# Start addresses of activation tiles, small tiles, and the weight ring in a two-block transformer layer

## What is computed

```
block 1: z = rmsnorm(x) @ w_in                      # "in": 36 tiles of 128 columns
         conv branch (31 taps), short conv branch   # -> a, s
         x += (g_a * (a @ w_a_out) + g_b * (s @ w_b_out)) @ w_o        # "a_out", "b_out", "o"
         u = rmsnorm(x) @ w_up; x += (gelu(conv(u1)) * u2) @ w_down    # "up", "down", hidden f
         x += sigmoid(rmsnorm(x) @ w_ple_gate) * (p @ w_ple)           # "gate", "ple"
block 2: qkv = rmsnorm(x) @ w_in_2                  # "in2", then attention -> y
         x += rmsnorm(y @ w_out_2)                                     # "out2"
         u = rmsnorm(x) @ w_up_2; f = gelu(conv(u1)) * conv(u2)        # "up2"
         x += rmsnorm(f @ w_down_2)                                    # "down2"
```

## Time and profile before

| | us |
|---|---|
| timed runs: median (lowest to highest) of 3 | 823.68 (821.07 to 823.71) |
| the profiled execution | 822.88 |
| its span, first to last instruction | 821.1 |
| TensorE busy | 779.7 (95%) |
| VectorE, ScalarE, GpSimd busy | 600.5, 449.6, 264.9 |
| DMA | 135.44 MB, mean 165 GB/s |

### The profile page before, as it was taken

The page is one execution under the profiler, slowest core; times in us unless marked ns, Lnnn a source line. Parts: engine busy times, 40 slices in busy tenths (PEclk is TensorE's granted clock), DMA queues, the critical chain, the costliest instruction groups (busy, mean ns, idle before and its releaser), DMA issues.

```text
span 821.1 us, 16957 instructions
## 1 busy us (share of the span) xinstructions
PE 779.7 (95%) x5954; PEld 748.8 (91%) x5954; DVE 600.5 (73%) x1058; ACT 449.6 (55%) x756; POOL 264.9 (32%) x160
## 2 busy tenths in 40 slices
PE   5989899899999999999899999699999999999996
PEld 5889899899999999999899998699999999988885
DVE  5899976767888888434957686479999999973333
ACT  7444354556565655444655564586666666653431
POOL 0366644464122212345563011642112221222220
PEclk9999999899999999999989999989999999999999
DMA  8445454455555557545433332525555555565551
GB/s 281 141 155 179 161 192 130 133 181 181 191 180 190 180 198 247 178 148 167 135 122 111 104 103 79 179 84 175 181 182 184 188 181 179 204 203 187 181 173 51
DMA packets 37771, 135.44 MB, mean 165 GB/s; under 512 B 4448, under 2 KB 4704, under 8 KB 37728
## 3 DMA queue, kind: packets, MB, share of 16 engines
q1 hardware_dynamic: 37728, 134.86, 49.7%
HBM read 133.80 MB, written 1.05 MB: 164 GB/s over the span
## 4 chain that ended last, share of the span: by engine, by line
PE 52%; DVE 3%; POOL 2%; issue 1%; ACT 1%; DVEq 0%; ACTq 0%; POOLq 0%
PE bank L1618 13%; PE bank L1619 12%; PE bank L1620 12%; PE bank L1948 4%; PE bank L1950 4%; PE bank L1949 4%; POOL sumsq L540 1%; PE bank L1823 1%; PE bank L1822 1%; DVE tmp L1382 1%; POOL X L658 1%; PE bank L1832 1%; DVE w_lo L1024 1%; PE bank L1640 0%; PE bank L1848 0%
## 5 line engine op out<-in xcount | busy, mean ns | idle before, releaser
L1618 PE MATMUL bank<-h_hi,w_hi 128*128 128x256 f32 x1424 | 410.7, 288 | 22.1 <-DVE h_lo L1036 13.4
L1619 PE MATMUL bank<-h_lo,w_hi 128*128 128x256 f32 x1424 | 406.4, 285 | 0.0
L1620 PE MATMUL bank<-h_hi,w_lo 128*128 128x256 f32 x1424 | 406.2, 285 | 0.0
L527 POOL TENSOR_TENSOR w_lo<-raw,w_hi 128x1024 fp32r<-128x1024 f32 (+2 forms) x78 | 192.9, 2477 | 407.4 <-ACT w_hi L684 407.4
L684 ACT ACTIVATE w_hi<-raw 128x1024 fp32r<-128x1024 f32 (+2 forms) x246 | 261.9, 1067 | 87.5 <-PE bank L1950 43.2
L1618 PEld LDWEIGHTS bank<-h_hi,w_hi 128*128 128x128 f32 x1424 | 276.7, 194 | 29.2 <-issue 21.3
L1024 DVE TENSOR_TENSOR w_lo<-raw,w_hi 128x1024 fp32r<-128x1024 f32 (+1 forms) x168 | 218.6, 1302 | 109.8 <-ACT w_hi L684 109.7
L1619 PEld LDWEIGHTS bank<-h_lo,w_hi 128*128 128x128 f32 x1424 | 277.1, 195 | 0.0
L1620 PEld LDWEIGHTS bank<-h_hi,w_lo 128*128 128x128 f32 x1424 | 276.8, 194 | 0.0
L1064 DVE TENSOR_TENSOR bank<-bank,scales 128x256 f32<-128x256 f32 x124 | 53.1, 431 | 37.3 <-PE bank L1620 29.5
L1291 DVE TENSOR_TENSOR f_lo<-src,f_hi 128x256 f32 (+1 forms) x54 | 58.7, 1086 | 0.5 <-ACT f_hi L831 0.5
(11 more groups left out here) (198 smaller groups left out, 924.3 us busy)
## 6 DMA issues: line engine op xcount, KB each, us to landing
raw<-in_w_up SPq DMA_DIRECT2D x108, 512.0 KB, 3.3
raw<-in_w_in SPq DMA_DIRECT2D x54, 512.0 KB, 3.4
...
```

The costliest lines, as they stand in the source:

```text
L527: nc.gpsimd.tensor_tensor(w_lo[s][:, 0:n], raw[s][:, 0:n], w_hi[s][:, 0:n].bitcast(f32), ALU.subtract).then_inc(lo_ready[s], 1)
L1618: nc.tensor.matmul(ps, wh, hi[:, k, :], start=start and n == 0, stop=False)
L1619: nc.tensor.matmul(ps, wh, lo[:, k, :], start=False, stop=False)
L1620: last = nc.tensor.matmul(ps, wl, hi[:, k, :], start=False, stop=stop and n == len(ks) - 1)
```

## The change

`at` now starts at (16481 + 31) // 32 * 32 = 16512, a multiple of 128. Tiles of 1024 bytes or more start at multiples of 64, smaller ones at multiples of 32. The small tiles come first, zeros and unused become two more columns of ones_over. Behind them the rings start 32 bytes past a multiple of 64 (past=RING_PAST), and everything behind the rings at multiples of 64. In down2, from its fourth unit on (first_col), a unit is loaded, rounded, subtracted and read from column 8 of the ring, 32 bytes further; the first three units, whose rounding the loop of up2 does, stay at column 0. For that SP loads the first four units of down2 ahead of the loop and the other 28 in seven passes of it instead of eight. Worked out with the sizes above, the tiles start at:

| start modulo 128 | before | after |
|---|---|---|
| raw, w_hi, w_lo | 32 | 96 |
| the same in down2, from its fourth unit | 32 | 96 + 32 = 0 |
| X, branch, h, h2, src, tmp, sq, sumsq, last_sq, scales | 32 | 0 |
| ev, cg, cv, f, gate, conv, q, k, v, score | 64 | 0 |
| s, a, mix, p | 96 | 64 |
| y_a, y_b, y | 0 | 64 |
| ident | 0 | 0 |

```diff
@@ -52,6 +52,13 @@
 RING = 4
 SQ_RING = 6
 LEAD = 3
+
+RING_PAST = 32
+
+
+def first_col(u):
+
+    return RING_PAST // 4 if u >= UNIT0["down2"] + LEAD else 0
 
 
 def unit_blocks(u):
@@ -253,43 +260,27 @@
 
     with ExitStack() as ctx:
         sem = lambda name: ctx.enter_context(nc.semaphore(name))
-        at = [(nc.sbuf_base + 63) // 32 * 32]
-
-        def sb(name, shape, dt=f32, offset=None):
+        at = [(nc.sbuf_base + 31) // 32 * 32]
+
+        def aligned(offset, size):
+            step = 64 if size >= 1024 else 32
+            return (offset + step - 1) // step * step
+
+        def sb(name, shape, dt=f32, offset=None, past=0):
 
             size = 4 * math.prod(shape[1:])
-            size = (size + 31) // 32 * 32
             if offset is not None:
                 return nc.alloc_sbuf_tensor_at(name, shape, dt, offset=offset)
+            at[0] = aligned(at[0] - past, size) + past
             t = nc.alloc_sbuf_tensor_at(name, shape, dt, offset=at[0])
             at[0] += size
             return t
 
-        UNIT_MAX = max(b for _, _, b in PHASES) * P
-        raw = [sb(f"raw{i}", [P, UNIT_MAX]) for i in range(RING)]
-        w_hi = [sb(f"w_hi{i}", [P, UNIT_MAX], f32r) for i in range(RING)]
-        w_lo = [sb(f"w_lo{i}", [P, UNIT_MAX], f32r) for i in range(RING)]
-        X = sb("X", [P, DC, TOK])
-        branch = sb("branch", [P, DC, TOK])
-        h_hi = sb("h_hi", [P, DC, TOK], f32r)
-        h_lo = sb("h_lo", [P, DC, TOK], f32r)
-        h2_at = at[0]
-        h2_hi, h2_lo = sb("h2_hi", [P, DC, TOK], f32r), sb("h2_lo", [P, DC, TOK], f32r)
-
-        o_gain = sb("o_gain", [P, 2, D], offset=h2_at)
-        post_gain = sb("post_gain", [P, D], offset=h2_at + 8 * D)
-        o_sq = sb("o_sq", [P, HALF], offset=h2_at + 12 * D)
-        src = [sb(f"src{i}", [P, TOK]) for i in range(2)]
-        tmp = [sb(f"tmp{i}", [P, TOK]) for i in range(4)]
-        sq = [sb(f"sq{i}", [P, TOK]) for i in range(SQ_RING)]
-        sumsq = sb("sumsq", [P, 2, TOK])
-        last_sq = sb("last_sq", [P, 2, TOK])
-        scales = sb("scales", [P, 2, TOK])
-        gg = sb("gg", [P, DC])
         vec = sb("vec", [P, N_VEC])
         ident = sb("ident", [P, P])
+        gg = sb("gg", [P, DC])
         g_first = sb("g_first", [P, DC])
-        ones_over = sb("ones_over", [P, P + 1])
+        ones_over = sb("ones_over", [P, P + 3])
         lsum = sb("lsum", [P, 2])
         lexp = sb("lexp", [P, 2])
         neg_lam = sb("neg_lam", [P, 1])
@@ -301,7 +292,28 @@
         minus_half = sb("minus_half", [P, 8])
         o_ss = sb("o_ss", [P, 2, 2])
         o_ms, o_rstd = sb("o_ms", [P, 2]), sb("o_rstd", [P, 2])
-        zeros, unused = sb("zeros", [P, 1]), sb("unused", [P, 1])
+        zeros, unused = ones_over[:, P + 1:P + 2], ones_over[:, P + 2:P + 3]
+
+        UNIT_MAX = max(b for _, _, b in PHASES) * P
+        raw = [sb(f"raw{i}", [P, UNIT_MAX], past=RING_PAST) for i in range(RING)]
+        w_hi = [sb(f"w_hi{i}", [P, UNIT_MAX], f32r, past=RING_PAST) for i in range(RING)]
+        w_lo = [sb(f"w_lo{i}", [P, UNIT_MAX], f32r, past=RING_PAST) for i in range(RING)]
+        X = sb("X", [P, DC, TOK])
+        branch = sb("branch", [P, DC, TOK])
+        h_hi = sb("h_hi", [P, DC, TOK], f32r)
+        h_lo = sb("h_lo", [P, DC, TOK], f32r)
+        h2_at = at[0]
+        h2_hi, h2_lo = sb("h2_hi", [P, DC, TOK], f32r), sb("h2_lo", [P, DC, TOK], f32r)
+
+        o_gain = sb("o_gain", [P, 2, D], offset=h2_at)
+        post_gain = sb("post_gain", [P, D], offset=h2_at + 8 * D)
+        o_sq = sb("o_sq", [P, HALF], offset=h2_at + 12 * D)
+        src = [sb(f"src{i}", [P, TOK]) for i in range(2)]
+        tmp = [sb(f"tmp{i}", [P, TOK]) for i in range(4)]
+        sq = [sb(f"sq{i}", [P, TOK]) for i in range(SQ_RING)]
+        sumsq = sb("sumsq", [P, 2, TOK])
+        last_sq = sb("last_sq", [P, 2, TOK])
+        scales = sb("scales", [P, 2, TOK])
         ev = [sb(f"ev{i}", [P, TOK]) for i in range(4)]
         cg_pair = sb("cg", [P, 2 * TOK])
         cg, y_sq = [cg_pair[:, i * TOK:(i + 1) * TOK] for i in range(2)], cg_pair
@@ -312,8 +324,10 @@
             at_ = [start]
 
             def place(name, shape, dt=f32):
+                size = 4 * math.prod(shape[1:])
+                at_[0] = aligned(at_[0], size)
                 t = sb(name, shape, dt, offset=at_[0])
-                at_[0] += (4 * math.prod(shape[1:]) + 31) // 32 * 32
+                at_[0] += size
                 assert at_[0] <= nc.sbuf_usable_end, (name, at_[0])
                 return t
             return place
@@ -460,12 +474,12 @@
 
         @block.sync
         def _(sp):
-            def load(name, i, wait):
+            def load(name, i, wait, col=0):
 
                 s, n = wait
                 if n is not None:
                     sp.wait_ge(lo_ready[s], n)
-                sp.dma_start(raw[s][:, 0:BLOCKS[name] * P],
+                sp.dma_start(raw[s][:, col:col + BLOCKS[name] * P],
                              d["w_" + name][ds(i, 1)].rearrange("a p n -> (a p) n")
                              ).then_inc(raw_in[s], 16)
 
@@ -490,12 +504,15 @@
             sp.dma_start(sinks[:], d["sinks"].partition_broadcast(P)).then_inc(const_in, 16)
             for name, units, _ in PHASES:
                 base = UNIT0[name]
-                first = RING if name == "in" else 0
+                first = RING if name in ("in", "down2") else 0
+                for i in range(first if name == "down2" else 0):
+                    load(name, i, (slot(base + i), (base + i) // RING), first_col(base + i))
                 full = (units - first) // RING
                 with sp.Fori(0, full, 1) as it:
                     for j in range(RING):
                         i = first + RING * it + j
-                        load(name, i, (slot(base + first + j), it + (base + first + j) // RING))
+                        load(name, i, (slot(base + first + j), it + (base + first + j) // RING),
+                             first_col(base + first + j))
                 for i in range(first + RING * full, units):
                     load(name, i, (slot(base + i), (base + i) // RING))
                 if name == "gate":
@@ -523,9 +540,10 @@
 
                 if u < N_UNITS and on_pool(u):
                     s, n = slot(u), (blocks or unit_blocks(u)) * P
+                    cols = slice(first_col(u), first_col(u) + n)
                     pool.wait_ge(hi_ready, RING * it + (u + 1))
-                    nc.gpsimd.tensor_tensor(w_lo[s][:, 0:n], raw[s][:, 0:n],
-                                            w_hi[s][:, 0:n].bitcast(f32), ALU.subtract
+                    nc.gpsimd.tensor_tensor(w_lo[s][:, cols], raw[s][:, cols],
+                                            w_hi[s][:, cols].bitcast(f32), ALU.subtract
                                             ).then_inc(lo_ready[s], 1)
 
             def add_square(name, c):
@@ -678,10 +696,11 @@
             def round_unit(u, it=0, blocks=None):
 
                 s, n = slot(u), (blocks or unit_blocks(u)) * P
+                cols = slice(first_col(u), first_col(u) + n)
                 act.wait_ge(raw_in[s], 16 * it + 16 * (u // RING + 1))
                 if u >= RING:
                     act.wait_ge(unit_done, RING * it + (u - RING + 1))
-                nc.scalar.activation(w_hi[s][:, 0:n], raw[s][:, 0:n], ACT.Copy).then_inc(hi_ready, 1)
+                nc.scalar.activation(w_hi[s][:, cols], raw[s][:, cols], ACT.Copy).then_inc(hi_ready, 1)
 
             def ahead(u):
                 if u + LEAD < N_UNITS:
@@ -722,7 +741,7 @@
 
             def load_table(function):
 
-                nc.scalar.activation(unused[:], zeros[:], function)
+                nc.scalar.activation(unused, zeros, function)
 
 
             act.wait_ge(memset_done, 1)
@@ -1020,9 +1039,10 @@
                 if on_pool(u):
                     return
                 s, n = slot(u), (blocks or unit_blocks(u)) * P
+                cols = slice(first_col(u), first_col(u) + n)
                 dve.wait_ge(hi_ready, RING * it + (u + 1))
-                nc.vector.tensor_tensor(w_lo[s][:, 0:n], raw[s][:, 0:n],
-                                        w_hi[s][:, 0:n].bitcast(f32), ALU.subtract
+                nc.vector.tensor_tensor(w_lo[s][:, cols], raw[s][:, cols],
+                                        w_hi[s][:, cols].bitcast(f32), ALU.subtract
                                         ).then_inc(lo_ready[s], 1)
 
             def ahead(u):
@@ -1073,7 +1093,7 @@
                                         ).then_inc(op_lo, 1)
 
 
-            nc.vector.memset(zeros[:], 0.0).then_inc(memset_done, 1)
+            nc.vector.memset(zeros, 0.0).then_inc(memset_done, 1)
             nc.vector.memset(ones_over[:, 0:P], 1.0 / D_CONF).then_inc(memset_done, 1)
             nc.vector.memset(ones_over[:, P:P + 1], 1.0 / D).then_inc(memset_done, 1)
             for i in (0, 1):
@@ -1941,10 +1961,11 @@
             with pe.Fori(1, FC2 // 2, 1) as it:
```

(7 more changed lines are left out.)

28 lines of the change are left out of this document (14 added, 14 removed).

## The result

The changed kernel takes 808.9 us at the median of four runs (808.8 to 809.7), the kernel before 822.8 (821.1 to 823.7) beside it on the same chip. The ratio is 0.984, its 95% interval 0.9825 to 0.9855: faster by 13.9 us. The prediction was 815.3, its range 811.8 to 819.7. The profiled execution took 809.7 us, its span 807.8; the span of before was 821.1, so 13.3 us are to be found.

The account below looks back on a forecast made before the run. The prediction took TensorE, through the distance between matmul starts, to bound the kernel. 3456 h matmuls at 2.2 ns less gave 7.6 us, all else 0: 822.9 - 7.6 = 815.3 us, range 811.8 to 819.7.

Parts of the forecast that it names:

- What bounds the kernel: TensorE, busy 95% of the span; a stage lasts its matmul count times the distance between starts, which the addresses set.
- Nothing moves: Rival: the h stages' 2.2 ns come from something else and the addresses only coincide; 822.9 us, chance 0.12.
- equal remainders modulo 128: Matmuls whose moving tile and weights start alike modulo 128 are slow, 120.0 ns; unequal pairs are fast, 117.8 to 118.3.
- The price of h: Products moving h or h2 fall from 120.0 to 117.8 ns: 2.2 ns on 3456 matmuls, 7.6 us gained.
- down2, put at 0 with bounds of -4.4 and +6.6 ns: Second down projection, 512 moving columns: no net change taken, -1.7 to +2.5 us possible on 384 matmuls.
- the prediction's own sign of being wrong: A distance in down2 moved from 233.4 by more than 2 ns, listed among what would show the prediction wrong.
- The equal-pair reading: In down2 the new pair (0, 0) has equal starts, so it would cost 0.8 us (384 x 2.2 ns).
- "s", "a", "p" at the fast distance already: The stages moving s, a and p already run at the fast distance, so they gain 0.
- "down" at 0: The first down projection, moving f, already runs at the fast distance of 117.8 ns and gains 0.
- Other engines: VectorE, ScalarE and GpSimd durations stay, cost 0; in "up2" VectorE's 10.1 free us cover the 3.4 us gain.
- a worse pair: Rival: in all h stages the new pair takes 122.2 ns, 7.6 us more, 830.5 us; chance 0.04.
- The range: 811.8 to 819.7 us: below, down2's gain, shorter waits and spread; above, VectorE leading "up2", with 1 us of spread.

Follow-up runs that it names:

- e3: The kernel before with only the weight rings moved 32 bytes down: 811.5 us, ratio 0.990 to before.
- e4: The kernel before with all activation tiles (X and all behind it) moved 32 bytes up, rings unmoved: 810.9 us, ratio 0.987 to before.
- e5: Network left out, only products in groups of 24 at all pairs of start addresses modulo 256 in 32-byte steps: 113.3 to 120.0 ns for 256 columns.
- e9: Network left out, 48 products at six address pairs behind 12 at each of eight distances, or pauses: distance 192 took 113.3 or 117.8 ns.
- e1: The changed kernel without the column shift, down2's units all stored from column 0: 811.3 us, ratio 0.988 to before.
- e2: The changed kernel with RING_PAST = 0, the rings at a multiple of 64: 819.6 us, ratio 0.998 to before.

## Why the prediction was wrong in size and right in direction

- **What bounds the kernel**: right. PE is still busy for all of "up" and "up2", a stage is its count times the distance of starts, and the start addresses set it. "Nothing moves" is refuted by e3 and e4, which move one group of tiles by 32 bytes and win 10 us. The Trainium skill (SBUF — State Buffer, "Who interferes with whom") calls PE's read ports for the moving operand and for LDWEIGHTS independent and says that PE never waits on anyone; that gives no cost to the addresses, and these runs disagree: 113.3 to 120.0 ns in e5 with nothing exchanged but the two operands' starts. Where in the machine the time goes no run shows.
- **The class "equal remainders modulo 128"**: the step that failed. Four values, 120.0, 117.8, 117.9 and 118.3, were sorted into one slow and one fast class. They were four points of a table by the distance modulo 256, in which distance 96, unequal modulo 128, is as slow as 0 (e5, e9). Of what the class put at zero, "down2", "down" and "s" to "a_out" changed. That the direction came out right owes something to luck: by the class any unequal pair would have been fast, and it is the new pair's distance of 32 that is; at 96, where s, a and p went, h would have stayed at 120.0.
- **The price of h**: mis-sized. I chose the row with the right coordinate, f at distance 32, and took its 117.8. Distance 32 has two values, and in after h runs at the other one, 116.7, in every long stretch on the path but "o"; why at that one no run shows. That is 3.3 ns instead of 2.2, on 3456 matmuls 11.5 us instead of 7.6, less 0.2 for "o". This is the largest part of the miss, 3.7 us.
- **down2, put at 0 with bounds of -4.4 and +6.6 ns**: wrong. It fell by 6.7 ns, out of bounds, worth 2.3 us; a move by more than 2 ns was the prediction's own sign of being wrong. The equal-pair reading had the sign wrong: with 512 moving columns distance 0 is the fastest (e1, e2, e5). A value for 256 columns says nothing of 512.
- **"s", "a", "p" at the fast distance already**: wrong. They went from distance 64 to 96 and from 117.8 to 120.0 ns, 0.5 us on 240 matmuls. The stretch from "s" to "a_out" still became 0.9 us shorter; its waits changed, and I haven't followed them.
- **"down" at 0**: 117.8 to 116.7, 0.6 us gained; f kept its distance of 32 and came to the other of its two values. y kept distance 224 and its 118.3: right.
- **The new sum**: 11.3 + 2.3 + 0.6 - 0.5 = 13.7 us, against 13.3 in the spans and 13.9 in the medians.
- **Other engines**: right. VectorE is busy for 154.28 of the 159.70 us of "up2" and its durations are unchanged. Neither it nor a worse pair took the gain.
- **The range** leant on the bounds from the rows of before. The unknown pairs got the spread of four known ones, and the space had eight distances and two widths. By its own terms the lower end is 815.3 - 1.7 - 1 - 1 = 811.6, not 811.8; the measured 808.9 lies below both.
